# Splitting the second layer's output projection rows during HGRN2's last head

## The chip, the cores and the metric

The kernel runs on one core of one Trainium2 chip. The metric is the device time of one execution in microseconds, as the median of several. The core's engines run side by side and wait for one another through semaphores: TensorE (PE, with its weight loads shown apart as PEld), VectorE (DVE), ScalarE (ACT), GpSimd (POOL), and SyncE (SP), which here only issues DMAs.

## What is computed

A trunk of two layers on 1024 tokens of width 1024, all in float32. Layer 0 has an RWKV-7 and an RG-LRU mixer; layer 1 has HGRN2. After each mixer comes an output projection with a residual add, and then a mixture of experts. The change lies where layer 1's mixer ends and its output projection begins:

```python
def hgrn2_mixer(hn, w_in, lower_bound, norm_w, w_out):
    q, f, i, g = jnp.split(hn @ w_in, 4, axis=-1)
    ...
    o = gla_chunkwise(split_heads(q, HGRN_HEADS), split_heads(k, HGRN_HEADS),
                      split_heads(i, HGRN_HEADS), split_heads(log_f, HGRN_HEADS))
    o = o * lax.rsqrt(jnp.mean(o * o, -1, keepdims=True) + RMS_EPS)
    o = o.reshape(b, s, HGRN_WIDTH) * norm_w * jax.nn.silu(g.astype(jnp.float32))
    return o.astype(hn.dtype) @ w_out

# layer 1
x = x + hgrn2_mixer(hn, c_w_in[j], lbs[layer], c_norm_w[j], c_w_out[j])
hn = rmsnorm(x, norm_ffn[layer])
x = x + hier_moe(hn, ...)
```

## The kernel before, in words

Every large product is made from three products in the fp32r format: each operand is split into a high part (a cast on ACT) and a low part (operand minus high part, a subtraction on DVE), and PE adds high x high, high x low and low x high into one PSUM bank. A weight row block of 128 x 1024 costs one cast and one subtraction.

The program is a row of phases (`phase`), each with one block of five instruction streams, one for each engine. The next block's streams begin when the streams of the last one have ended. Within an engine the order is that of the code. Two phases matter here.

**`hgrn`** (layer 1's mixer) handles 8 heads. For each head, PE computes the four projections q, f, i, g of the normed input `h_T` (high part) and `h_low` (low part) with the head's weight columns. SP fetches these to `w_tiles`, ACT and DVE split them to `w_high` and `w_low`. `step` handles the rest of a head: the products within chunks on seven levels (`level_gram`; DVE makes the exponents with `diff`, ACT exponentiates them with `level_exp`, DVE scales with `scale` and picks results with `pick`), then the transposes of `k_to_end` (`turn`, L2050), the products of keys and values (L2078), the chain of states on DVE (L2315), the output products (L2087, L2088), the square on ACT (L2178), the sums of squares (L2093), their mean on DVE (L2324), a logarithm and an exponential on ACT (L2183, L2184), and two products on DVE (L2331, L2336), the last of which writes the head's rows of `y_T`. While a head goes through `step`, PE fills its waits with the projections of the following head: `project(n)` issues 3n of these matmuls. In the last head (`more` is False) there is no following head, so `project` issues nothing, and neither `w_tiles`, `w_high`, `w_low` nor `h_T`, `h_low` are read any more.

**`moe`** with layer 1's arguments starts with the output projection. SP issues eight DMAs for the rows of `c_w_out` (L1326, to `w_raw`), alternating with eight for the rows of the residual (L1328), and then the norm's gain (L1329) and the router's weights and biases (L1330 to L1333). ACT casts the first 128 tokens of `y_T` (`y_part`, L1440) and then the eight weight row blocks to `wo_high` (L1529); DVE makes the low parts (L1718 and L1780). PE's `project(t, h)` computes half h of the projected token tile t with 24 matmuls (L1574): eight high x high, eight x_low x high, eight x high x low. In tile 0, half 0, it waits for each row block as it comes. Then each tile's result is added to the residual (`add`, L1725, whose first one also waits for the gain), squared on ACT, normed (`rows`, L1730), turned on PE (`turn_rows`, L1595) and multiplied by the router's weights (`logits`, L1605). PE's order is `project(0,0)`, `project(0,1)`, `project(1,0)`, `turn_rows(0)`, `project(1,1)`, `logits(0)`, and so on, up to tile 7. The routing and the experts follow.

Layer 0's `moe` has the same code with one difference (`early`): its output projection rows are already in SBUF, so SP begins with the residual's DMAs. The splits are still made in the phase.

The line of `moe` that holds PE's first tile to the rows:

```python
if t == 0 and h == 0 and ready is not None:
    pe.wait_ge(ready, k + 1)
```

## Time and profile before

| what | us |
|---|---|
| median of 3 runs | 2879.13 (2876.95 to 2888.28) |
| the profiled execution, own time | 2883.18 |
| its span, first to last instruction | 2881.4 |
| PE busy in the span | 2555.6 (89%) |
| DVE busy | 1927.9 (67%) |
| ACT busy | 1603.9 (56%) |

Times in the profile are measured from the span's start. "Idle before" in brackets is the time the engine had nothing to do before the row's instruction, with what ended it; a name ending in q is the engine's own instruction queue, which stands for a semaphore wait.
### The profile page before, as it was taken

How to read it: one execution, taken by the hardware profiler on the slowest of the kernel's cores; microseconds unless marked ns; L12 is line 12 of the kernel's file. 1: busy time of each engine (PE TensorE's matmuls, PEld its weight loads, DVE VectorE, ACT ScalarE, POOL GpSimd, SP SyncE). 2: the span in 40 equal slices, each digit the busy share in tenths (PEclk: the TensorE clock that was granted, in tenths of full speed). 3: DMA queues.
4: the chain of work that ended last, by engine and by line, in shares of the span. 5: the costliest groups of instructions: out<-in, count | busy, mean ns of one | idle time of the engine just before them, and what ended most of it. 6: DMA issues, size and time to landing. Idle time of an engine off the chain costs nothing. (4 is left out here: it accounts for less than half of the span.)

```text
span 2881.4 us, 57941 instructions
## 1 busy us (share of the span) xinstructions
PE 2555.6 (89%) x20860; PEld 2090.6 (73%) x20860; DVE 1927.9 (67%) x2201; ACT 1603.9 (56%) x1867; POOL 379.6 (13%) x342
## 2 busy tenths in 40 slices
PE   5998899979989999999568999997597999999990
PEld 4776799847768888888457777776485788888870
DVE  3358356534479999999545666666335899999974
ACT  3656223253248888888324655554222788888861
POOL 0020000000013333333010000000000122222220
PEclk9999999989989999999779999998797999999995
DMA  3111000013269999999520111110323899999964
GB/s 95 45 44 30 27 4 4 4 60 127 88 231 377 385 382 383 382 375 378 198 72 26 36 38 37 32 31 9 141 75 123 329 376 376 382 383 387 381 256 188
DMA packets 219991, 525.39 MB, mean 182 GB/s; under 512 B 43824, under 2 KB 99120, under 8 KB 219824
## 3 DMA queue, kind: packets, MB, share of 16 engines
q1 hardware_dynamic: 201392, 489.34, 45.8%
q0 software_dynamic: 18432, 33.60, 3.1%
q8 instruction: 132, 2.16, 0.3%
q14 instruction: 35, 0.29, 0.0%
HBM read 506.06 MB, written 50.33 MB: 193 GB/s over the span
## 5 line engine op out<-in xcount | busy, mean ns | idle before, releaser
L1751 DVE TENSOR_TENSOR w_low<-w_raw,w_high 128x1024 fp32r<-128x1024 f32 x768 | 894.8, 1219 | 31.3 <-DVEq L52 21.7
L1464 ACT CAST w_high<-w_raw 128x1024 fp32r<-128x1024 f32 x768 | 755.1, 1049 | 109.1 <-ACTq L52 108.7
L1619 PE MATMUL ps<-w_high,x_high 128*128 128x512 f32 x1024 | 415.0, 405 | 7.5 <-PEq L52 6.6
L1623 PE MATMUL ps<-w_high,x_low 128*128 128x512 f32 x1024 | 404.0, 395 | 0.0
L1622 PE MATMUL ps<-w_low,x_high 128*128 128x512 f32 x1024 | 401.9, 393 | 0.0
L1619 PEld LDWEIGHTS ps<-w_high,x_high 128*128 128x128 f32 x1024 | 195.5, 191 | 50.6 <-issue 14.0
L1623 PEld LDWEIGHTS ps<-w_high,x_low 128*128 128x128 f32 x1024 | 194.2, 190 | 43.4
L2013 PE MATMUL ps<-h_high,w_high 128*128 128x512 f32 x512 | 213.4, 417 | 10.8 <-PEq L52 10.5
L1622 PEld LDWEIGHTS ps<-w_low,x_high 128*128 128x128 f32 x1024 | 195.0, 190 | 37.7
L1619 PE MATMUL ps<-w_high,hidden_high 128*128 128x512 f32 x512 | 200.7, 392 | 6.7 <-PEq L52 6.7
L2013 PE MATMUL ps<-h_high,w_low 128*128 128x512 f32 x512 | 201.9, 394 | 0.0
L2013 PE MATMUL ps<-h_low,w_high 128*128 128x512 f32 x512 | 201.7, 394 | 0.0
L1623 PE MATMUL ps<-w_high,hidden_low 128*128 128x512 f32 x512 | 200.5, 392 | 0.0
L1622 PE MATMUL ps<-w_low,hidden_high 128*128 128x512 f32 x512 | 200.4, 391 | 0.0
L1410 POOL COPY row_index<-place_of_row 128x1 int32 (+1 forms) x64 | 104.2, 1629 | 676.7 <-POOLq L52 676.7
L1469 ACT CAST x_high<-ps 128x1024 fp32r<-128x1024 f32 x64 | 65.0, 1016 | 182.3 <-ACTq L52 182.3
L1412 POOL DMA_INDIRECT expert_rows<-y_rows,row_index x64 | 155.2, 2425 | 56.4 <-POOLq L52 56.4
L263 PE MATMUL ps<-h_high,w_high 128*128 128x512 f32 x352 | 143.2, 407 | 15.5 <-DVE w_low L527 10.8
L1755 DVE TENSOR_TENSOR x_low<-ps,x_high 128x1024 fp32r<-128x1024 f32 x64 | 78.4, 1224 | 105.4 <-DVEq L52 105.4
L263 PE MATMUL ps<-h_high,w_low 128*128 128x512 f32 x352 | 140.5, 399 | 0.0
L263 PE MATMUL ps<-h_low,w_high 128*128 128x512 f32 x352 | 139.9, 397 | 0.0
L1379 POOL IOTA iota_moe<- 128x128 f32 x2 | 0.5, 238 | 1035.2 <-POOLq L1975 559.7
(402 smaller groups left out, 4865.6 us busy)
## 6 DMA issues: line engine op xcount, KB each, us to landing
w_raw<-in_moe_w_gate SPq DMA_DIRECT2D x256, 512.0 KB, 5.2
w_raw<-in_moe_w_up SPq DMA_DIRECT2D x256, 512.0 KB, 5.6
w_raw<-in_moe_w_down SPq DMA_DIRECT2D x256, 512.0 KB
w_raw<-expert_rows SPq DMA_DIRECT2D x32, 512.0 KB, 9.1
w_tiles<-in_c_w_in SPq DMA_DIRECT2D x32, 512.0 KB, 4.0
w_tiles<-in_ab_w_in SPq DMA_DIRECT2D x22, 512.0 KB, 3.9
residual<-in_x SPq DMA_DIRECT2D x16, 512.0 KB, 7.3
h_rows<-hn_moe SPq DMA_DIRECT2D x16, 512.0 KB, 2.9
```

The costliest lines, as they stand in the source:

```text
L263: last = pe.matmul(ps[:, bank(i) + h, :], wx_[:, i % 2, q, :], hx[:, q, tok], start=n == 0, stop=n == len(parts) - 1)
L1379: ch(pool.iota(it, [[1, P]], base=0, channel_multiplier=0, allow_small_or_imprecise_dtypes=True))
L1410: pool.tensor_copy(idx[:, 1:2], dst_row[:, b]).then_inc(order_p, 1)
L1412: pool.indirect_dma_start(c.ys, bass.IndirectOffsetOnAxis(ap=idx[:, 1:2], axis=0), yb, None, bounds_check=2 * S - 1, oob_is_err=False).the ...
L1464: act.copy(wh[:, p, :], raw[:, p, :]).then_inc(high_made, 1)
L1469: act.copy(xh[:, q], ps[:, B_X:B_X + 2, :].rearrange("p b (k n) -> p (b k) n", k=4)).then_inc(order_a, 1)
L1619: ins = pe.matmul(ps[:, bank, :], high, w_h, start=first, stop=False)
L1622: pe.matmul(ps[:, bank, :], high, w_l, start=False, stop=False)
L1623: return pe.matmul(ps[:, bank, :], low, w_h, start=False, stop=final)
L1751: dve.tensor_tensor(wl[:, p, :], raw[:, p, :], wh[:, p, :].bitcast(F32), ALU.subtract).then_inc(low_made, 1)
L1755: dve.tensor_tensor(xl[:, q], ps[:, B_X:B_X + 2, :].rearrange("p b (k n) -> p (b k) n", k=4), xh[:, q].bitcast(F32), ALU.subtract).then_in ...
L2013: last = pe.matmul(ps[:, 2 * (m % 2) + h, :], wx[:, m % 2, k, :], hx[:, k, tok], start=n == 0, stop=n == len(parts) - 1)
```

## The change

`hgrn` gets `w_out`. A ring of five row buffers (`w_out_ring`) is laid over `w_tiles`, `w_high` and `w_low`. PE signals `w_dead` with the first transpose of the last head's v, which comes after the last projection matmul; SP then fetches the rows 0 to 4, and the rows 5 to 7 as their slots come free (after the low part of rows 0 to 2). In the last head's `step`, ACT casts the rows at seven places to the high part, into `h_T`, and DVE makes the low parts at two places, into `h_low`. `moe` takes these two tensors (`split`) in place of `wo_high` and `wo_low`, and neither fetches, splits nor waits for rows. In the last head, `project` now issues one float32 matmul of 128 x 512 into PSUM bank 0, whose result nobody reads, at each of its 12 places.

```diff
--- before.py
+++ after.py
@@ -1202,7 +1202,7 @@
 
-def moe(nc, c, a, layer, y, w_out, next_gain, fetch=None, early=False, h_high=None, h_low=None, out=None):
+def moe(nc, c, a, layer, y, w_out, next_gain, fetch=None, early=False, split=None, h_high=None, h_low=None, out=None):
 
@@ -1279,6 +1279,8 @@
         w_rows = c.w_out_rows if early else raw
+        if split is not None:
+            wo_h, wo_l = split
         at_pos, reach, at_blk = at["at_pos"], at["reach"], at["at_block"]
@@ -1322,7 +1324,7 @@
                 for k in range(KT):
-                    if not early:
+                    if not early and split is None:
                         sp.dma_start(raw[:, k, :], w_out[k * P:(k + 1) * P, :]).then_inc(raw_in[k], 16)
@@ -1334,7 +1336,8 @@
                     sp.dma_start(c.rows[t * P:(t + 1) * P, :], hn[:, t % 2, :]).then_inc(rows_in[t % 2], 16)
-                    sp.wait_ge(wo_low, t + 1)
+                    if split is None:
+                        sp.wait_ge(wo_low, t + 1)
                     load(slice(0, 1), [t], fresh=True)
@@ -1521,7 +1524,7 @@
                 y_part(0)
-                for k in range(KT):
+                for k in range(KT if split is None else 0):
                     if early:
@@ -1569,7 +1572,7 @@
                         for k in range(KT):
-                            if t == 0 and h == 0 and ready is not None:
+                            if t == 0 and h == 0 and ready is not None and split is None:
                                 pe.wait_ge(ready, k + 1)
@@ -1775,7 +1778,7 @@
                 y_rest(0)
-                for k in range(KT):
+                for k in range(KT if split is None else 0):
                     dve.wait_ge(wo_high, k + 1)
@@ -1911,7 +1914,7 @@
 
-def hgrn(nc, c, w, lower_bound, norm_w, h_T, h_low, y_T):
+def hgrn(nc, c, w, lower_bound, norm_w, h_T, h_low, y_T, w_out):
 
@@ -1932,8 +1935,14 @@
         gram_done, gram_free = [sem("gram_done0"), sem("gram_done1")], [sem("gram_free0"), sem("gram_free1")]
+
+        RING = 5
+        with nc.sbuf_tensor("w_out_ring", [P, RING, D], F32) as ring:
+            pass
         wt = sb("w_tiles", [P, KT, P])
         wh, wl = sb("w_high", [P, 2, KT, P], F32R), sb("w_low", [P, 2, KT, P], F32R)
+        w_dead, out_high, out_low = sem("w_dead"), sem("out_high"), sem("out_low")
+        out_in = [sem(f"out_in{k}") for k in range(KT)]
         Q, G, V, F = c.head_rows
@@ -1998,6 +2007,11 @@
                 sp.wait_ge(s["par_in"], 48)
+                sp.wait_ge(w_dead, 1)
+                for k in range(KT):
+                    if k >= RING:
+                        sp.wait_ge(out_low, k - RING + 1)
+                    sp.dma_start(ring[:, k % RING, :], w_out[k * P:(k + 1) * P, :]).then_inc(out_in[k], 16)
 
@@ -2045,20 +2059,27 @@
 
-                def turn(src, done):
+                def turn(src, done, first=None):
                     for n in range(TT):
                         last = pe.transpose(ps[:, 6 + n // 4, (n % 4) * P:(n % 4 + 1) * P], src[:, n * P:(n + 1) * P], c.ident[:])
+                        if n == 0 and first is not None:
+                            last.then_inc(first, 1)
                     last.then_inc(done, 1)
 
-                def turn_v(par):
+                def turn_v(par, first=None):
                     take(pe, s["v_ready"])
                     take(pe, s["tail_free"])
-                    turn(V[:, par, :], s["v_turned"])
-
-                def step(par, more):
+                    turn(V[:, par, :], s["v_turned"], first)
+
+                def step(par, more, final=False):
                     ahead = projection() if more else iter(())
+                    if not more:
+                        take(pe, bank_free[0])
 
                     def project(n):
+                        if not more:
+
+                            pe.matmul(ps[:, 0, :], c.ident[:], Q[:, par, 0:HALF], start=True, stop=True)
                         for _ in range(3 * n):
@@ -2094,7 +2115,7 @@
                     if more:
-                        turn_v(1 - par)
+                        turn_v(1 - par, w_dead if final else None)
 
@@ -2102,7 +2123,7 @@
                     step(1, True)
-                step(0, True)
+                step(0, True, final=True)
                 step(1, False)
@@ -2150,23 +2171,36 @@
 
+                def row_high(*ks):
+                    for k in ks:
+                        act.wait_ge(out_in[k], 16)
+                        act.copy(h_T[:, k, :], ring[:, k % RING, :]).then_inc(out_high, 1)
+
                 def step(par, more, ahead=True):
...
                     level_exp(4)
+                    if not more:
+                        row_high(0)
                     level_exp(5)
+                    if not more:
+                        row_high(1)
                     if more:
...
                         level_exp(lv)
+                    if not more:
+                        row_high(2)
                     take(act, s["diff_ready"])
...
                         high(3)
+                    if not more:
+                        row_high(3, 4)
                     take(act, s["kd_turned"])
@@ -2174,8 +2208,12 @@
                             high(0)
+                    if not more:
+                        row_high(5, 6)
                     take(act, s["o_done"])
                     act.activation(KD[:], pair(ps[:, 4:6, :]), ACT.Square).then_inc(s["sq_ready"], 1)
+                    if not more:
+                        row_high(7)
                     if more:
@@ -2285,6 +2323,11 @@
 
+                def row_low(*ks):
+                    for k in ks:
+                        dve.wait_ge(out_high, k + 1)
+                        dve.tensor_tensor(h_low[:, k, :], ring[:, k % RING, :], h_T[:, k, :].bitcast(F32), ALU.subtract).then_inc(out_low, 1)
+
                 def step(h, par, more, ahead=True):
@@ -2309,6 +2352,8 @@
                     dve.tensor_tensor(QE[:], QE[:], Q[:, par, :], ALU.mult).then_inc(s["qe_ready"], 1)
+                    if not more:
+                        row_low(0, 1)
                     take(dve, s["ds_done"])
@@ -2320,6 +2365,8 @@
                             low(0)
+                    if not more:
+                        row_low(*range(2, KT))
                     take(dve, s["sq_summed"])
@@ -2394,8 +2441,8 @@
         with nc.sbuf_tensor("hgrn_y_h", [P, 3 * KT, S], F32):
-            hgrn(nc, c, a["c_w_in"][0], a["c_lower_bound"], a["c_norm_w"][0], h_T, h_low, y_T)
-        moe(nc, c, a, 1, y_T[:], a["c_w_out"][0], a["norm_final"], fetch=c.res_rows, out=out)
+            hgrn(nc, c, a["c_w_in"][0], a["c_lower_bound"], a["c_norm_w"][0], h_T, h_low, y_T, a["c_w_out"][0])
+        moe(nc, c, a, 1, y_T[:], a["c_w_out"][0], a["norm_final"], fetch=c.res_rows, split=(h_T, h_low), out=out)
         with nc.Block() as block:
...
```

Where instructions move, in three places.

PE, last head of `hgrn` (v, q, k, level_ops, k_to_end, v_rows, scores_T and states are that head's tensors; the row of `q,ident` is the new matmul). Before:

```order
L2024 MATMUL ps<-q,k 128x128 x8
L2038 MATMUL ps<-level_ops 64x64 x8
L2038 MATMUL ps<-level_ops 32x32 x16
L2044 MATMUL ps<-level_ops 32x16 x160
L2050 MATMUL ps<-ident,k_to_end 128x128 x8
L2078 MATMUL ps<-v_rows,k_rows 128x128 x8
L2087 MATMUL ps<-scores_T,v_rows 128x128
```

and with the change, in two pieces (between them the pattern of level and new matmul repeats):

```order
L2038 MATMUL ps<-q,k 128x128 x8
L2082 MATMUL ps<-q,ident 128x512
L2052 MATMUL ps<-level_ops 64x64 x8
L2082 MATMUL ps<-q,ident 128x512
L2052 MATMUL ps<-level_ops 32x32 x16
L2082 MATMUL ps<-q,ident 128x512
L2058 MATMUL ps<-level_ops 32x16 x32
```

```order
L2082 MATMUL ps<-q,ident 128x512
L2064 MATMUL ps<-ident,k_to_end 128x128 x8
L2082 MATMUL ps<-q,ident 128x512
L2099 MATMUL ps<-v_rows,k_rows 128x128 x8
L2082 MATMUL ps<-q,ident 128x512
L2108 MATMUL ps<-scores_T,v_rows 128x128
```

A new matmul now stands before each level, before the transposes, before the key-value products and before the output products; two more stand before and behind the sums of squares.

ACT, from the last head's level exponentials to the next phase. Before:

```order
L2165 ACTIVATE k_to_end<-k_to_end 128x1024
L2166 ACTIVATE q_from_start<-cum_log_f 128x1024
L2171 COPY k_rows<-ps 128x1024
L2178 ACTIVATE k_to_end<-ps 128x1024
L2183 ACT_TABLE_LOAD
L2183 ACTIVATE log_f<-log_f 128x1024
L2184 ACT_TABLE_LOAD
L2184 ACTIVATE log_f<-log_f 128x1024
L1975 UNCONDITIONAL_BRANCH
L1435 UNCONDITIONAL_BRANCH
L1440 CAST x_high<-y_T 128x1024
L1529 CAST wo_high_moe<-w_raw 128x1024 x8
```

and with the change:

```order
L2177 CAST h_high<-w_out_ring 128x1024
L2197 ACTIVATE k_to_end<-k_to_end 128x1024
L2198 ACTIVATE q_from_start<-cum_log_f 128x1024
L2177 CAST h_high<-w_out_ring 128x1024 x2
L2205 COPY k_rows<-ps 128x1024
L2177 CAST h_high<-w_out_ring 128x1024 x2
L2214 ACTIVATE k_to_end<-ps 128x1024
L2177 CAST h_high<-w_out_ring 128x1024
L2221 ACT_TABLE_LOAD
```

The eight casts have moved ahead of the block's end; the first two of them stand still further ahead, between level exponentials.

DVE, the same stretch. Before:

```order
L2311 TENSOR_TENSOR q_from_start<-q_from_start,q 128x1024
L2315 SCALAR_TENSOR_TENSOR states<-states,step_decay,ps 128x128 x7
L2324 TENSOR_SCALAR log_f<-ps 128x1024
L2331 SCALAR_TENSOR_TENSOR log_f<-ps,norm_w,log_f 128x1024
L2336 TENSOR_TENSOR y_T<-log_f,g 128x1024
L1975 UNCONDITIONAL_BRANCH
L1706 UNCONDITIONAL_BRANCH
L1718 TENSOR_TENSOR x_low<-y_T,x_high 128x1024
L1780 TENSOR_TENSOR wo_low_moe<-w_raw,wo_high_moe 128x1024 x8
```

and with the change:

```order
L2354 TENSOR_TENSOR q_from_start<-q_from_start,q 128x1024
L2329 TENSOR_TENSOR h_low<-w_out_ring,h_high 128x1024 x2
L2360 SCALAR_TENSOR_TENSOR states<-states,step_decay,ps 128x128 x7
L2329 TENSOR_TENSOR h_low<-w_out_ring,h_high 128x1024 x6
L2371 TENSOR_SCALAR log_f<-ps 128x1024
```

Two subtractions now stand ahead of the chain of states, six behind it and ahead of the mean of squares.

## Rows read from the trace of the kernel before

**Rows 1.** Timeline of PE, the output projection of layer 1: start, duration, row

```profile
2047.44 0.76 PE L1574 MATMUL ps<-wo_high_moe,x_high 128*128 128x512 f32 x1 [14.94 <-ACT wo_high_moe L1529]
...
2065.28 0.79 PE L1574 MATMUL ps<-wo_high_moe,x_high 128*128 128x512 f32 x1 [1.78 <-ACT wo_high_moe L1529]
...
2070.62 1.98 PE L1574 MATMUL ps<-wo_high_moe,x_high 128*128 128x512 f32 x8
...
2076.06 1.98 PE L1574 MATMUL ps<-wo_high_moe,x_high 128*128 128x512 f32 x8
...
2081.51 1.03 PE L1595 MATMUL ps<-ident,hn_moe 128*128 128x128 f32 x8
```

**Rows 2.** Timelines of SP, DVE and ACT, start of layer 1's `moe`

```profile
2042.52 0.35 SPq L1326 DMA_DIRECT2D w_raw<-in_c_w_out  x1
...
2043.62 1.23 DVE L1718 TENSOR_TENSOR x_low<-y_T,x_high 128x1024 fp32r<-128x1024 f32 x1 [1.59 <-ACT x_high L1440]
...
2048.82 1.04 ACT L1529 CAST wo_high_moe<-w_raw 128x1024 fp32r<-128x1024 f32 x1 [1.53 <-ACTq L52]
```

**Rows 3.** Stretches: length, busy us (instructions) of PE, PEld, DVE, ACT, POOL, PEclk, DMA share, GB/s

```profile
2023.50:2027.00 3.50, 3.17 (x15) 3.20 (x16) 0.00 (x0) 0.00 (x0) 0.00 (x0) 0.50 0.02 5
2046.00:2065.00 19.00, 5.52 (x7) 2.00 (x7) 8.58 (x7) 8.13 (x8) 0.59 (x1) 0.50 1.03 413
2068.00:2071.00 3.00, 3.00 (x14) 2.48 (x13) 0.12 (x1) 0.00 (x0) 0.00 (x0) 0.97 0.04 6
2226.40:2231.90 5.50, 5.50 (x13) 4.32 (x14) 1.23 (x1) 1.07 (x2) 0.00 (x0) 0.50 0.17 60
```

**Rows 4.** Layer 0's `moe`, first transfers and first add (timelines of SP and DVE)

```profile
651.86 3.93 SPq L1328 DMA_DIRECT2D residual<-in_x  x8
...
666.99 0.69 DVE L1725 TENSOR_TENSOR residual<-residual,ps 128x512 f32<-128x512 f32 x1 [2.50 <-DMA gain_rows_moe<-in_norm_ffn]
```

**Rows 5.** Timeline of PE, the last head

```profile
2011.52 1.06 PE L2044 MATMUL ps<-level_ops 128*32 128x16 f32 x64 [2.21 <-PEq L52]
2012.51 1.97 PE L2050 MATMUL ps<-ident,k_to_end 128*128 128x128 f32 x8
2015.75 3.75 PE L2078 MATMUL ps<-v_rows,k_rows 128*128 128x128 f32 x16 [1.27 <-PEq L52]
2023.83 0.77 PE L2087 MATMUL ps<-scores_T,v_rows 128*128 128x128 f32 x2 [4.33 <-PEq L52]
...
2030.54 1.95 PE L2093 MATMUL ps<-k_to_end,ones 128*128 128x512 f32 x4 [1.29 <-PEq L52]
```

**Rows 6.** Timelines of ACT and DVE, the last head

```profile
2005.94 0.69 ACT L2136 ACTIVATE level_ops<-level_ops 128x512 f32<-128x512 f32 x1 [1.80 <-ACTq L52]
2029.38 1.02 ACT L2178 ACTIVATE k_to_end<-ps 128x1024 f32<-128x1024 f32 x1 [13.77 <-ACTq L52]
...
2019.77 3.31 DVE L2315 SCALAR_TENSOR_TENSOR states<-states,step_decay,ps 128x128 f32<-128x128 f32 x7 [2.99 <-DVEq L52]
2032.65 1.22 DVE L2324 TENSOR_SCALAR log_f<-ps 128x1024 f32<-128x1024 f32 x1 [9.57 <-DVEq L52]
```

**Rows 7.** The page's DMA issues: KB each, median us from issue to landing

```profile
w_tiles<-in_c_w_in SPq DMA_DIRECT2D x32, 512.0 KB, 4.0
```

**Rows 8.** Timeline of PE: float32 matmuls of 128 x 512, and a level product, elsewhere

```profile
625.47 1.91 PE L786 MATMUL ps<-residual,head_ones 128*128 128x512 f32 x2
...
1937.87 0.74 PE L2044 MATMUL ps<-level_ops 128*32 128x16 f32 x64
...
2188.31 10.46 PE L1677 MATMUL ps<-residual,ones 128*128 128x512 f32 x24
```

**Rows 9.** Stretches with PE partly busy (columns as in rows 3)

```profile
617.00:621.00 4.00, 1.49 (x4) 0.68 (x4) 2.13 (x3) 3.94 (x5) 0.00 (x0) 0.99 0.00 0
621.00:622.00 1.00, 1.00 (x2) 0.00 (x0) 0.06 (x1) 1.00 (x1) 0.00 (x0) 0.50 0.00 0
644.80:648.00 3.20, 1.48 (x4) 0.38 (x2) 2.19 (x3) 3.15 (x4) 0.00 (x0) 1.00 0.00 0
```

## The prediction

> **What bounds the kernel now.** The page gives PE 89% of the span, so I first ask where PE waits, and read the waits by engine for the stretch around the change. The largest of PE there stands in [rows 1]: the projection of layer 1 starts at 2047.44 after 14.94 us of idleness, and its first eight matmuls then come one by one, the last at 2065.28, each released by a cast. Only from 2065.28 does PE run densely; the second half of tile 0 starts at 2070.62 and tile 1 at 2076.06. Then I read ACT and DVE. ACT's casts take 1.04 us and stand 1.53 us idle before each, waiting for a queue [rows 2]. The table of stretches says what they wait for: from 2046 to 2065 the DMA engines are fully busy at 413 GB/s, PE is busy for 5.52 of 19 us and its clock is at the lower level [rows 3]. So the start of the projection is bound by the transfer of 4.2 MB of weight rows, which alternate with 4.2 MB of residual. The first tile's operand is ready much earlier, at 2043.62 + 1.23 = 2044.85 [rows 2]. From 2076 on PE is dense, and everything behind it (router, experts) is started by what PE and the norm deliver.
>
> The other half of the change lies in the last head. There PE waits for DVE and ACT (idle 2.21 us before a level product of 1.06 us), so each of the last levels takes the 3.27 us that DVE needs [rows 5]. From 2012.51 the head is a chain of PE, ACT and DVE in turn [rows 5, 6]: transposes, copy, key-value products (to 2019.5), states (to 2023.1), output products (to 2029.3), square, sums (to 2032.5), mean. Any delay in it delays the phase's end.
>
> **Step 1, the projection's start.** Fetch, casts and subtractions leave the phase. PE can start when the operand is split, 2044.95. Half a tile is 24 matmuls; at the upper clock they cost 2076.06 - 2070.62 = 5.44 us [rows 1], tile 0 therefore 10.9 us. The clock is at the lower level at the start, since PE has been idle for over 10 us. How long it stays there I take from three places: dense from 2065.28, at the upper level for nearly all of 2068 to 2071 (about 2.8 us); dense from 2023.5, lower until 2027.0 (3.5 us); dense from 2226.4, lower for all of 5.5 us [rows 3]. A matmul takes about twice as long there, so c us at the lower level cost c/2. With the middle of 2.8 and 5.5, c = 4.2: tile 0 takes 13.0 us, and tile 1 starts at 2057.95 where it started at 2076.06. **Saving 18.1 us**, between 17.4 (c = 5.5) and 18.8 (c = 2.8).
>
> What is late next? The first add waits for the gain, which is queued behind the residual. Layer 0 has just this order of transfers without weight rows: first issue 651.86, the add released by the gain at 666.99, 15.1 us later [rows 4]. Here the first issue is at 2042.52 [rows 2], so the first add starts at 2057.65 and ends at 2058.35, 0.4 us after tile 0's second half is done. PE needs the normed rows only for its transposes behind the first half of tile 1, which came without a wait at 2081.51 [rows 1], 5.45 us after tile 1's start. That path has a few tenths of slack, so I take **0.1 us** of loss, between 0 and 1. The router's weights and biases stand behind the gain in the queue; the logits need them only after tile 1's second half, at about 2069, some 11 us after the gain, so I cost them at nothing.
>
> **Step 2, casts and subtractions in the last head.** Costs are 1.04 us each on ACT and 1.22 us on DVE. The rows 0 to 4 are asked for at 1986, when v's transposes begin, and land some 4 us later [rows 7], long before the first cast at about 2001. ACT idles 1.80 us between level exponentials and 13.77 us before the square [rows 6], so the first seven casts are covered: nothing. DVE idles 2.99 us before the states and 9.57 us before the mean [rows 6]: two subtractions (2.4 us) fit in the first gap, six (7.4 us) in the second. Rows 5, 6 and 7 are asked for when their slots are free, at about 2018, 2019 and 2024; with 4 us they land by 2022, 2023 and 2028. The cast of row 7 stands behind the square (2030.4), its subtraction ends at 2032.7, against 2032.65 for the mean now. Cost 0.1 us while the head keeps its pace; if the head gets faster, row 7 takes some of that gain.
>
> **Step 3, the twelve added matmuls.** One is two instructions: 0.87 us at the upper clock (10.46 us for 24 instructions), 1.7 us at the lower (two in 1.91 us, which includes the fill) [rows 8]. Seven stand before the levels, where PE idles 2.21 us [rows 5]: covered, even at 1.9. The eighth stands between the last level and the transposes, which now start without a gap at 2012.51 [rows 5]; it is exposed in full. The ninth has 1.27 us of cover, the tenth 4.33, the eleventh 1.29 [rows 5], the twelfth delays nobody. What they do to the clock decides. Now it is at the lower level until 2027.0 [rows 3], and the whole of this chain up to the output products runs there.
>
> - Clock stays up: the last level's product takes 0.74 us instead of 1.06 and ends 0.3 us sooner, the eighth matmul takes 0.87, the transposes 1.0 instead of 1.97, the key-value products 1.9 instead of 3.75 [rows 5], done at 2017.4. Now DVE's two subtractions are late next: they end at 2019.2, so states start 0.5 us sooner than 2019.77. The output products take 3.8 us instead of 5.5 (2023.83 to 2029.38 [rows 5, 6]), together 2.1 us sooner. Row 7's subtraction (landing 2028, cast, 1.2 us) gives back 0.3: **1.8 us gained**.
> - Clock falls as before: the eighth matmul costs 1.7 and the ninth 0.4, against a clock that opens sooner behind the denser run from 2011.5. Between 1.1 gained and 2.1 lost; I take 0.6 lost.
>
> In the stretch from 617 to 621 PE was busy 37% of the time and the clock was at the lower level right after it, from 621; from 644.8 to 648 it was busy 46% and the clock stayed up [rows 9]. With the new matmuls a level of 3.27 us holds 0.87 + 0.74 us of PE [rows 8], 49%, though almost half of that in tiles of 32 columns. That is above both rows, so I take the clock as staying up. The page "TensorE: Matmul & The Clock Gate" of the Trainium skill (section "HAM oscillation — how this bites in real kernels") puts the fall down to idle gaps alone. The row from 617 disagrees in part, since PE was idle for only 2.5 of its 4 us; by the page the sum is that of the first case, by that row the second has to be reckoned with.
>
> **Sum.** 18.1 - 0.1 + 1.8 = 19.8 us. The profiled execution took 2883.18 us and so comes to 2863.4. It lies 4.05 us above the median of the runs; from 2879.13 the same saving gives **2859.3 us**.
>
> **Rivals.**
> - *A, the forecast*: 2859.3, between 2858.0 (18.8 + 2.3) and 2861.
> - *B, the clock falls in the last head*: 18.1 - 0.1 - 0.6 = 17.4, 2861.7; ends 15.3 and 19.8, so 2859.3 to 2863.8. For it speaks the row from 617 and that the level products use narrow tiles; against it the row from 644.8.
> - *C, the transfers at the phase's head decide*: gain or router weights land 3 to 6 us later than in layer 0, because reading back the residual is slower than reading x. PE then waits before its transposes, and the saving is 12 to 15: 2864 to 2867. Against it: 413 GB/s was reached here with the same transfers in the mix.
> - *D, the change hides what was hidden*: if the experts' first weights or the routing set the end of the stage by a clock of their own, the 18 us vanish and 2877 to 2880 remains. Against it: each of these loads is issued by a wait on the normed rows, so it moves along.
> - *E, slower*: the ring. Row 7 is asked for at 2024 by the end of row 2's subtraction, and the mean waits behind its subtraction on DVE. A landing of L us costs L - 6, and the change turns slower when L exceeds 6 + 18 = 24 us; a landing of 40 would give 2895. Against it: a landing of 4 us in this phase with the queue empty, as it is here [rows 7].
>
> **How the numbers follow.** Chances: A 0.50, B 0.35, C 0.07, D 0.06, E 0.02. A saving over 0.5% is one over 14.4 us, about what a measurement of this kernel can tell from no change. A and B save 15 to 21, but the runs of before spread over 11 us, so the measured medians may put a saving of 17 below the bound; I leave 0.06 of A and B for that, and 0.02 of C above it. Faster 0.81, within 0.5% 0.17, slower 0.02. The range takes in A and B with their ends (2858.0 to 2863.8), 4 us below for the spread of the runs' median (2876.95 is the fastest run before), and above as far as C: 2854 to 2868.
>
> **What would show it.** Right: first projection matmul some 3 us after the last row of `y_T` and 24 dense ones behind it; PEclk 1.00 through the levels; the mean of squares 1.5 to 2 us sooner than 2032.65; no idle PE before the first transposes of the normed rows. B shows as PEclk 0.50 in the levels. C shows as an add released by the gain and idle PE behind tile 1's first half. Wrong: a wait of ACT or DVE for rows inside the head, or a time between 2872 and 2880.

## The result, and the profile after

The change made the kernel faster by about 0.6%, as forecast: the median of 5 runs is 2864.53 us (2860.32 to 2867.0) against 2881.68 us (2876.95 to 2888.28, 5 runs) for the kernel before. The ratio is 0.994, with a 95% interval of 0.9927 to 0.9954, and the medians differ by 17.15 us. The forecast was a saving of 19.8 us and 2859.3 us; the measured time lies in the range of 2854 to 2868.

The interval of the ratio is some 8 us wide, and unchanged code alone moves by several us between two executions: up to v's transposes of the last head the profiled execution before took 1985.77 us, the one after 1989.64. So I split each profiled execution at marks that every kernel has:

- the **head**: from the start of the last head's v transposes to the end of the last `y_T` row;
- the **start**: from there to tile 1's first projection matmul; the first transposes of normed rows follow 5.45 us later unless PE has to wait.

| us | before | after | difference |
|---|---|---|---|
| up to the last head | 1985.77 | 1989.64 | +3.87 |
| head | 56.27 | 56.09 | -0.18 |
| start | 34.02 | 15.49 | -18.53 |
| tile 1 to the span's end | 805.34 | 803.68 | -1.66 |
| span | 2881.4 | 2864.9 | -16.5 |

What the change touches saved 18.7 us; the other two rows are code that is the same in both kernels.

The timeline of PE after the change, from the last level of the last head to the first transposes of normed rows (start, duration, row), answers to [rows 1, 5]:

```profile
2015.43 0.73 PE L2058 MATMUL ps<-level_ops 128*32 128x16 f32 x64 [1.49 <-PEq L52]
2016.08 1.13 PE L2082 MATMUL ps<-q,ident 128*128 128x512 f32 x2
2017.04 1.04 PE L2064 MATMUL ps<-ident,k_to_end 128*128 128x128 f32 x8
2017.92 1.02 PE L2082 MATMUL ps<-q,ident 128*128 128x512 f32 x2
2019.36 2.02 PE L2099 MATMUL ps<-v_rows,k_rows 128*128 128x128 f32 x16 [0.41 <-PEq L52]
2021.21 1.02 PE L2082 MATMUL ps<-q,ident 128*128 128x512 f32 x2
2026.94 0.77 PE L2108 MATMUL ps<-scores_T,v_rows 128*128 128x128 f32 x2 [4.70 <-PEq L52]
...
2048.59 3.68 PE L1577 MATMUL ps<-h_high,x_high 128*128 128x512 f32 x8 [11.54 <-DVE x_low L1721]
2052.11 2.02 PE L1577 MATMUL ps<-h_high,x_low 128*128 128x512 f32 x8
...
2061.22 1.98 PE L1577 MATMUL ps<-h_high,x_high 128*128 128x512 f32 x8
...
2066.67 1.03 PE L1598 MATMUL ps<-ident,hn_moe 128*128 128x128 f32 x8
```

The projection now waits for its operand alone and runs its 24 matmuls of each half in a row; the first eight take 3.5 us at the lower clock, then the short ones begin. Up to the key-value products the head runs at the upper clock (1.04 and 2.02 us, against 1.97 and 3.75 in [rows 5]). Then PE idles for 4.70 us, and the first pair of output products takes 0.77 us as before.

DVE and ACT after the change, the same stretch (answers to [rows 2, 4, 6]):

```profile
2020.61 2.35 DVE L2329 TENSOR_TENSOR h_low<-w_out_ring,h_high 128x1024 fp32r<-128x1024 f32 x2
2022.88 3.30 DVE L2360 SCALAR_TENSOR_TENSOR states<-states,step_decay,ps 128x128 f32<-128x128 f32 x7
...
2035.06 1.22 DVE L2329 TENSOR_TENSOR h_low<-w_out_ring,h_high 128x1024 fp32r<-128x1024 f32 x1 [2.86 <-ACT h_high L2177]
2036.34 1.23 DVE L2371 TENSOR_SCALAR log_f<-ps 128x1024 f32<-128x1024 f32 x1
...
2060.88 1.28 DVE L1728 TENSOR_TENSOR residual<-residual,ps 128x512 f32<-128x512 f32 x2 [11.12 <-DMA gain_rows_moe<-in_norm_ffn]
```

```profile
2025.20 1.04 ACT L2177 CAST h_high<-w_out_ring 128x1024 fp32r<-128x1024 f32 x1 [5.99 <-DMA w_out_ring<-in_c_w_out]
2027.78 1.05 ACT L2177 CAST h_high<-w_out_ring 128x1024 fp32r<-128x1024 f32 x1 [1.53 <-DMA w_out_ring<-in_c_w_out]
2033.07 1.02 ACT L2214 ACTIVATE k_to_end<-ps 128x1024 f32<-128x1024 f32 x1 [4.25 <-ACTq L52]
```

The states start behind two low parts, without a gap: DVE, not the key-value products (done at 2021.4), now sets their start. ACT waits for rows 5 and 6, but has 4.25 us to spare before the square. Row 7 has nothing to spare: its low part ends at 2036.28, PE's sums of squares at 2036.19, and the mean starts at 2036.34. The first add waits for the gain, until 15.15 us after `y_T`, and PE's transposes come without a wait all the same.

The stretches of the head (columns as in [rows 3]) show the clock:

```profile
2016.00:2020.00 4.00, 3.58 (x36) 2.23 (x25) 3.30 (x4) 2.01 (x3) 0.00 (x0) 1.00 0.00 0
2020.00:2024.00 4.00, 2.24 (x15) 1.41 (x13) 3.71 (x6) 0.00 (x0) 0.00 (x0) 1.00 0.23 67
2024.00:2028.00 4.00, 1.06 (x5) 1.09 (x6) 3.17 (x7) 1.27 (x2) 0.00 (x0) 0.59 0.57 196
2028.00:2032.00 4.00, 4.00 (x22) 4.00 (x22) 4.00 (x4) 0.82 (x1) 0.00 (x0) 0.56 0.42 135
```

It is up through the levels and the key-value products, and falls soon after 2024, in PE's idle gap behind them. That it stayed up through the levels is not certain even with the twelve added matmuls, as the section on e8 shows.

### The profile page after: what moved, and what is told of

Same layout as the page of the kernel before. It is cut to its first block and busy times, and to the rows that moved or that the text cites. A ratio compares the mean times of both kernels' runs of the same rounds, so it can differ in the third digit from the quotient of the medians.

```text
span 2864.9 us, 57992 instructions
## 1 busy us (share of the span) xinstructions
PE 2560.0 (89%) x20884; PEld 2091.0 (73%) x20884; DVE 1927.5 (67%) x2201; ACT 1603.4 (56%) x1867; POOL 381.3 (13%) x342
```

## The experiments

The profiled head, start and time up to the first transposes, by the marks above, with the ratio to the kernel before and its 95% interval:

| kernel | ratio | head | start | to transposes |
|---|---|---|---|---|
| before | 1 | 56.27 | 34.02 | 39.47 |
| the change | 0.994 (0.9927 to 0.9954) | 56.09 | 15.49 | 20.94 |
| e1 no added matmuls | 0.994 (0.9927 to 0.9953) | 57.31 | 15.77 | 21.22 |
| e2 added matmuls alone | 0.9998 (0.9989 to 1.0008) | 55.52 | 34.61 | 40.06 |
| e3 rows' transfers first | 0.9966 (0.9953 to 0.9979) | 56.52 | 26.32 | 31.76 |
| e4 three more matmuls | 0.9937 (0.9922 to 0.9951) | 55.52 | 15.76 | 21.21 |
| e5 filler up to the start | 0.9924 (0.9907 to 0.994) | 54.42 | 17.02 | 22.47 |
| e6 e5, gain first | 0.9928 (0.9914 to 0.9941) | 54.07 | 15.81 | 21.26 |
| e7 one low part ahead | 0.9921 (0.9901 to 0.9942) | 54.39 | 16.03 | 21.48 |
| e8 low parts on GpSimd | 0.9935 (0.9919 to 0.9951) | 61.48 | 15.44 | 21.30 |
| e9 fetch alone | 0.9957 (0.9943 to 0.997) | 57.40 | 20.72 | 26.17 |
| e10 low parts behind | 0.9922 (0.9909 to 0.9936) | 52.75 | 16.77 | 22.21 |
| e11 e10 and the start | 0.9929 (0.9915 to 0.9942) | 52.72 | 13.91 | 19.35 |
| e12 e10's order, no filler | 0.9933 (0.992 to 0.9946) | 57.34 | 15.76 | 21.42 |

An interval is 0.2 to 0.4% wide, 5 to 12 us. So the times tell the change from before and from e2. The interval of e3 only touches that of the change, that of e9 overlaps it, and the variants of the head can't be told from one another. Those are read from the profiles, one of each, and there a head can differ by about a microsecond for how long the clock was down alone: with the same output products and no added matmul, it took 56.27 (before), 56.52 (e3), 57.31 (e1), 57.34 (e12) and 57.40 us (e9).

### e1: the change without the added matmuls

```diff
                     def project(n):
-                        if not more:
-
-                            pe.matmul(ps[:, 0, :], c.ident[:], Q[:, par, 0:HALF], start=True, stop=True)
                         for _ in range(3 * n):
```

> The change without its twelve added matmuls; everything else stays. Two stretches are read in the profile: the head (from the start of v's transposes to the end of the last y_T row, 56.3 us before, 56.1 with the change) and the start (from there to tile 1's first projection matmul, 34.0 before, 15.5 with the change). Theory: the gain is all in the start, so the start stays at 15 to 16 us and the total stays within 1 us of the change's. The head then runs its levels at the lower clock as before: 56.3 to 56.9. Rival (the added matmuls carry part of the gain by keeping the clock up): the head gets longer by 1.8 us or more, 57.9 or above.

The ratio is that of the change. The head ran as before up to its output products (states at 2015.42, 33.9 us after v's transposes; 34.0 before), with five casts and two low parts already done. From the square on it took 12.66 us, as before, so the other casts and low parts are covered too. Between the two it took 6.66 us from the first output product to the square, where the kernel before took 5.55 and the change 6.13. That is the clock, which in e1 opened 5.7 us after the dense run began and before it opened after 3.2. So the theory's 56.3 to 56.9 was passed by 0.4, and the rival's 57.9 not reached. The head with the added matmuls is 1.2 us shorter in this pair of profiles, but kernels without them differ by as much among themselves (56.27 to 57.40), and the times show nothing.

### e2: the added matmuls alone, in the kernel before

```diff
+                    if not more:
+                        take(pe, bank_free[0])
                     def project(n):
+                        if not more:
+                            pe.matmul(ps[:, 0, :], c.ident[:], Q[:, par, 0:HALF], start=True, stop=True)
                         for _ in range(3 * n):
```

> The kernel before plus only the twelve added matmuls. The start must stay at 34 us in every theory. Theory (the clock falls in the gap before the output products because DVE's two subtractions and the states keep PE idle there): without the subtractions DVE is ready for the states sooner, PE's idle gap is about 1.5 us shorter; if that is enough to keep the clock up, the head takes 56.3 - 2.1 - 1.5 = 52.5 to 53.5; if not, the states still come sooner and the head takes 54 to 55. Rival (the added matmuls give nothing by themselves): 56 to 57.

PE's timeline in e2:

```profile
2010.43 2.02 PE L2083 MATMUL ps<-v_rows,k_rows 128*128 128x128 f32 x16 [0.41 <-PEq L52]
2012.29 1.02 PE L2066 MATMUL ps<-q,ident 128*128 128x512 f32 x2
2016.81 0.77 PE L2092 MATMUL ps<-scores_T,v_rows 128*128 128x128 f32 x2 [3.50 <-PEq L52]
```

The output products start 36.1 us after v's transposes, 1.2 sooner than with the change (37.3): without the two low parts DVE begins the states sooner. PE still idles for 3.50 us and still comes back at the lower clock, and stays there for 5.7 us, so of 2 us gained ahead of the output products 0.75 remain: the head takes 55.52, between theory (55 at most) and rival. In the times nothing is seen (0.9998).

### e3: the weight rows' transfers ahead of the residual's, in the kernel before

```diff
                 for k in range(KT):
                     if not early:
                         sp.dma_start(raw[:, k, :], w_out[k * P:(k + 1) * P, :]).then_inc(raw_in[k], 16)
+                for k in range(KT):
                     if fetch is not None:
```

> The kernel before with the eight weight row transfers issued ahead of the eight residual transfers, nothing else. If the start is bound by the transfer, rows land every 1.3 us in place of 2.56, the eighth by about 2055, tile 0 ends some 10 us sooner; the gain is still behind all 8.4 MB (landing at 2067) and holds the first add. So the start shrinks from 34.0 to 24 to 25 us, and PE then waits about 1 to 2 us before its first transposes: total 8 to 9 us less, half of what the change gives. Rival (the casts and subtractions in the phase cost the time, not the transfer): the start stays within 2 us of 34.

The casts of the rows in e3, against 1.53 us of idleness before each in [rows 2]:

```profile
2048.22 1.04 ACT L1530 CAST wo_high_moe<-w_raw 128x1024 fp32r<-128x1024 f32 x1 [0.22 <-ACTq L52]
2049.50 1.04 ACT L1530 CAST wo_high_moe<-w_raw 128x1024 fp32r<-128x1024 f32 x1 [0.24 <-ACTq L52]
```

Rows now come about every 1.3 us. The start shrank by 7.7 us, to 26.32 where 24 to 25 was expected; a microsecond of that is the clock, since from the last row's first matmul to tile 1 it took 11.77 us in place of 10.78. The run shrank by 0.34%, somewhat over half of what the change gives, from one line of order. So the transfer bound the start, and a good part of that was that a row waited behind residual that nobody needed yet. The wait for the gain was there (the first add at 25.36 us, released by it), but cost PE nothing: the transposes came 5.44 us after tile 1's start.

### e9: the fetch alone

```diff
+                sp.wait_ge(w_dead, 1)
+                for k in range(KT):
+                    sp.dma_start(c.raw_rows[:, k, :], w_out[k * P:(k + 1) * P, :]).then_inc(c.w_out_in[k], 16)
...
-        w_rows = c.w_out_rows if early else raw
+        w_rows = c.w_out_rows if early else raw if rows_at is None else rows_at[:]
```

> The kernel before with only the fetch moved: all eight rows are fetched during the last head into SBUF that is no longer read (the low part of the normed input), and cast and subtracted in the next phase as before; no added matmuls. Theory: the change's gain in the start is mostly the transfer. The start is then like layer 0's, where the rows are in SBUF too: about 20.6 us from y_T to tile 1 (34.0 before, 15.5 with the change), so the moved fetch is worth 13.4 us and the moved splits the other 5. The head stays at 56.3 to 57.4. Rival (splits and transfer are equally binding, so the fetch alone gives little): 28 us or more.

20.72 us, against 20.6 read from layer 0. So of the 18.5 us in the start the moved fetch brings 13.3 and the moved splits 5.2. With the rows in SBUF, ACT's casts set the pace (one matmul every 0.95 us):

```profile
2047.63 0.79 PE L1574 MATMUL ps<-wo_high_moe,x_high 128*128 128x512 f32 x1 [0.15 <-ACT wo_high_moe L1529]
2048.58 0.79 PE L1574 MATMUL ps<-wo_high_moe,x_high 128*128 128x512 f32 x1 [0.15 <-ACT wo_high_moe L1529]
```

### e4: three more matmuls ahead of the output products

```diff
+                    for _ in range(3 if not more else 0):
+                        pe.matmul(ps[:, 0, :], c.ident[:], Q[:, par, 0:HALF], start=True, stop=True)
                     take(pe, s["s_ready"])
```

> The change plus three more of the added matmuls ahead of the last head's output products. Theory (the output products ran at the lower clock because PE idled 4.7 us before them): the idle gap shrinks to about 2 us, PEclk stays 1.00, the output products take 3.8 us in place of 6.0, and row 7's fetch and cast become late: the head takes 54.3 to 55 us in place of 56.1. Rival (row 7's fetch bounds the mean of squares anyway): the head stays at 55.8 or above. The start stays at 15 to 16 us in both.

```profile
2022.37 0.46 PE L2110 MATMUL ps<-scores_T,v_rows 128*128 128x128 f32 x2 [2.14 <-PEq L52]
2022.67 0.39 PE L2111 MATMUL ps<-q_from_start,states 128*128 128x128 f32 x2
...
2023.34 0.43 PE L2110 MATMUL ps<-scores_T,v_rows 128*128 128x128 f32 x2
2023.56 0.64 PE L2111 MATMUL ps<-q_from_start,states 128*128 128x128 f32 x2
...
2026.98 0.39 PE L2111 MATMUL ps<-q_from_start,states 128*128 128x128 f32 x2
```

The clock was still up when the output products began, and fell in their midst at 2023.5, 1.2 us after PE had come back from only 2.14 us of idleness, to be up again at 2026.98: 5.56 us for them, the head 55.52, and the theory's 54.3 to 55 missed. PE had not idled since, so I take the fall to answer, late, to the idleness before; no run here excludes another cause. e8 shows the same: after 3.47 us of idleness its output products began at the upper clock at 2027.87 and turned slow at 2028.39. The page "TensorE: Matmul & The Clock Gate" of the Trainium skill (section "HAM oscillation — how this bites in real kernels") tells of it as a wait that is followed by a cold run. Here a run that began warm turned cold while it was dense.

### e7: one low part ahead of the states

```diff
-                        row_low(0, 1)
+                        row_low(0)
...
-                        row_low(*range(2, KT))
+                        row_low(*range(1, KT))
```

> The change with one subtraction in place of two ahead of the last head's chain of states, the other behind it. Theory (with the clock up the key-value products are done 1.5 us before DVE is): the states start about 1.1 us sooner, 32.1 us after v's transposes in place of 33.2, and the idle gap of PE before the output products shrinks to 3.5 us; row 6 and row 7 land later but before they're needed, so the head takes 54.7 to 55.3 us, if the clock opens within the output products at the same point. Rival (a later fetch of rows 6 and 7 takes the gain): 55.9 or more, with ACT waiting for a row in front of the square.

States at 32.08 us after v's transposes, as forecast. With an idle gap of 3.57 us in place of 4.70 the clock stayed up this time, and the output products took 3.8 us. The rival holds too: row 6 was asked for later, ACT stood before it, and the square behind it (the output products were done at 2028.17, so it could have begun at 2028.3):

```profile
2029.01 1.04 ACT L2177 CAST h_high<-w_out_ring 128x1024 fp32r<-128x1024 f32 x1 [4.18 <-DMA w_out_ring<-in_c_w_out]
2029.96 1.02 ACT L2214 ACTIVATE k_to_end<-ps 128x1024 f32<-128x1024 f32 x1
```

Of 3.4 us gained ahead of the square 1.7 were given back there; the head took 54.39, a little below the expected 54.7 to 55.3, which had not counted on the clock.

### e8: the low parts of rows 0 to 2 on GpSimd

```diff
+                for k in range(3):
+                    pool.wait_ge(out_high, k + 1)
+                    pool.tensor_tensor(h_low[:, k, :], ring[:, k, :], h_T[:, k, :].bitcast(F32), ALU.subtract).then_inc(pool_low, 1)
...
-                        sp.wait_ge(out_low, k - RING + 1)
+                        sp.wait_ge(pool_low, k - RING + 1)
...
-                        row_low(0, 1)
...
-                        row_low(*range(2, KT))
+                        row_low(*range(3, KT))
```

> The change with the low parts of rows 0, 1 and 2 made by GpSimd, as soon as ACT has cast them, in place of DVE; SP waits for these for the rows 5 to 7, and DVE makes the low parts of rows 3 to 7 behind the states. Theory (DVE's order sets the states and the fetch of the last rows): the states start right after the key-value products, 31.7 to 32.0 us after v's transposes; rows 5 to 7 are in SBUF before the output products begin, and nothing waits for them; head 53.5 to 55. Rival (GpSimd's subtractions slow DVE's in the levels, where DVE is fully busy): the levels take longer than 3.27 us each, and the head takes 56 or more.

The rival, and far beyond it: the head took 61.48 us. GpSimd and DVE in e8:

```profile
2000.64 3.00 POOL L1992 TENSOR_TENSOR h_low<-w_out_ring,h_high 128x1024 fp32r<-128x1024 f32 x1 [519.61 <-ACT h_high L2180]
2004.01 2.38 POOL L1992 TENSOR_TENSOR h_low<-w_out_ring,h_high 128x1024 fp32r<-128x1024 f32 x1 [0.37 <-ACT h_high L2180]
```

```profile
1998.66 0.68 DVE L2309 TENSOR_TENSOR level_ops<-level_ops,k 128x512 f32<-128x512 f32 x1
...
2001.33 0.73 DVE L2294 COPY_PREDICATED scores_T<-level_masks,ps 128x512 f32<-128x512 uint32 x1
2001.93 2.26 DVE L2309 TENSOR_TENSOR level_ops<-level_ops,k 128x512 f32<-128x512 f32 x1
2004.43 2.50 DVE L2314 TENSOR_TENSOR level_ops<-level_ops,q 128x512 f32<-128x512 f32 x1 [0.24 <-DVEq L52]
```

A DVE multiplication that takes 0.68 us takes 2.26, 2.50 and, at the third subtraction, 2.25 us when it meets GpSimd, and ends 0.54 to 0.56 us after the end of GpSimd's instruction each time, however long they overlap: it looks like a wait, not a slowdown. The copy ahead of the first, which reads PSUM and one SBUF tensor, takes its usual 0.73. The three lengthened multiplications cost DVE 5.0 us. The page "GPSIMD Engine Reference" of the Trainium skill (section "Key points") says that the two engines share their SBUF interfaces, with contention for DVE instructions that have two SBUF inputs. The rows agree, and show its size.

The rest of the head's loss is the clock, and it fell in the levels, before GpSimd did anything. PE in e8:

```profile
1997.30 0.87 PE L2061 MATMUL ps<-level_ops 128*32 128x16 f32 x64 [3.15 <-PEq L52]
1998.09 2.08 PE L2085 MATMUL ps<-q,ident 128*128 128x512 f32 x2
...
2018.20 1.92 PE L2067 MATMUL ps<-ident,k_to_end 128*128 128x128 f32 x8
```

The added matmul takes 2.08 us in place of 1.12 at 1998.09, GpSimd's first subtraction starts at 2000.64. The transposes are cold too (1.92 us, 1.04 in the change), and the states start 39.19 us after v's transposes, 7.2 us later than where nothing of DVE stands in front of them (e2, 32.01): 5.0 for GpSimd, some 2.2 for the lower clock. The same fall is in the levels of e5, e6, e7, e10 and e11, whose code is that of the change up to there: for 6 to 14 us their added matmuls took up to 2.08 us and their level products up to 1.06. There the clock was up again before the transposes and the states started no later for it, since DVE sets the pace of the levels. Only in the change, e2 and e4 was it up all through. So of nine profiles with the added matmuls, six have the fall that they were meant to prevent.

### e10: low parts behind the states and behind the mean

```diff
-                        row_low(0, 1)
+                        row_low(0)
...
-                        row_low(*range(2, KT))
+                        row_low(*range(1, 6))
...
                     dve.sem_inc(s["tail_free"], 1)
+                    if not more:
+                        row_low(6, 7)
...
-                        row_high(5, 6)
+                        row_high(5)
...
-                        row_high(7)
+                        row_high(6, 7)
...
+                    for _ in range(3 if not more else 0):
+                        pe.matmul(ps[:, 0, :], c.ident[:], Q[:, par, 0:HALF], start=True, stop=True)
                     take(pe, s["s_ready"])
```

> The change with another order in the last head: one low part ahead of the states, those of rows 1 to 5 behind them, those of rows 6 and 7 behind the mean of squares, where DVE idles 5.2 us; ACT casts row 5 ahead of the square, rows 6 and 7 behind it; and three more added matmuls ahead of the output products. Theory: states start 32.1 us after v's transposes, output products 36.1 to 40.0 at the upper clock, nothing of ACT or DVE waits for a row, the mean of squares comes at 43.3, and the head takes 52.6 to 53 us (56.1 with the change): 3.3 us less in total. Rival (something else in the tail binds, such as ACT's casts ahead of the logarithm): 54 or more.

States at 32.1 us, output products at 36.17, square at 40.10, mean at 43.37, head 52.75: each within 0.15 us of the forecast, 3.3 less than with the change. ACT did wait for rows 5 and 7 (6.04 and 0.55 us), which cost nothing. DVE in e10:

```profile
2018.79 5.76 DVE L2331 TENSOR_TENSOR h_low<-w_out_ring,h_high 128x1024 fp32r<-128x1024 f32 x5 [0.24 <-DVEq L52]
2026.51 1.22 DVE L2373 TENSOR_SCALAR log_f<-ps 128x1024 f32<-128x1024 f32 x1 [1.96 <-DVEq L52]
2028.07 2.36 DVE L2331 TENSOR_TENSOR h_low<-w_out_ring,h_high 128x1024 fp32r<-128x1024 f32 x2 [0.33 <-DVEq L52]
2032.94 1.28 DVE L2382 SCALAR_TENSOR_TENSOR log_f<-ps,norm_w,log_f 128x1024 f32<-128x1024 f32 x1 [2.51 <-DVEq L52]
```

The mean waits for PE's sums alone, and the last two low parts lie in DVE's wait for ACT's logarithm and exponential. In the times, 2855.5 us (2852.45 to 2860.06) and 0.9922; the interval overlaps that of the change.

### e12: e10's order without filler

Against e10:

```diff
                     def project(n):
-                        if not more:
-
-                            pe.matmul(ps[:, 0, :], c.ident[:], Q[:, par, 0:HALF], start=True, stop=True)
                         for _ in range(3 * n):
...
-                    for _ in range(3 if not more else 0):
-                        pe.matmul(ps[:, 0, :], c.ident[:], Q[:, par, 0:HALF], start=True, stop=True)
                     take(pe, s["s_ready"])
```

> e10's order of casts and low parts, without any added matmul. Theory (order and filler act together: at the lower clock the key-value products end 33.7 us after v's transposes, after DVE's lows in either order, so the order alone frees nothing): states start at 33.9 to 34.0 as before, output products at 38.0, and the head takes 56.3 to 57.4 us as in e1, the spread being how long the output products stay at the lower clock; total within 0.1% of e1's ratio 0.994. Rival (the order alone carries e10's gain): head 54 or less.

The head took 57.34 us, like e1's 57.31. At the lower clock the key-value products end at 33.7 us, and DVE is done by then with what stands ahead of the states, two low parts in e1 or one here. So the order pays only with the filler. The filler hardly pays with twelve matmuls or fifteen (the change, e4), but in the change's own order, with six more ahead of the output products and no gap left there, the head takes 54.42 and 54.07 (e5, e6, next section): the states start at 33.2 as with the change, and the output products take 3.9 us. The gain over the change there is the clock alone; e10's is clock and order.

### e5, e6 and e11: keeping the clock up for the projection

e5, against the change:

```diff
                     project(8)
+                    for _ in range(6 if not more else 0):
+                        pe.matmul(ps[:, 0, :], c.ident[:], Q[:, par, 0:HALF], start=True, stop=True)
                     take(pe, s["s_ready"])
...
                     project(9)
+                    for _ in range(7 if not more else 0):
+                        pe.matmul(ps[:, 0, :], c.ident[:], Q[:, par, 0:HALF], start=True, stop=True)
...
+                for _ in range(3 if split is not None else 0):
+                    pe.matmul(ps[:, 2, :], c.ones[:], y[:, 0, 0:HALF], start=True, stop=True)
                 for t in range(TT):
                     project(t, 0)
```

e6, against e5; e11 makes the same edit to e10 and adds the last two loops of the diff above, with 9 and 2 matmuls in place of 7 and 3:

```diff
+                if split is not None:
+                    sp.dma_start(gb, gain.partition_broadcast(P)).then_inc(gain_in, 16)
                 for k in range(KT):
...
-                sp.dma_start(gb, gain.partition_broadcast(P)).then_inc(gain_in, 16)
+                if split is None:
+                    sp.dma_start(gb, gain.partition_broadcast(P)).then_inc(gain_in, 16)
```

> The change plus added matmuls in every longer idle stretch of PE up to the projection: six ahead of the output products (e4 had three), seven behind the sums of squares, three at the head of the next phase. Theory (what the output products and tile 0 lose at the lower clock is given back by filler, but the gain's transfer is late next): the head takes 54.0 to 54.8 us; tile 0's matmuls take 10.9 us in place of 12.6, but the first add still waits for the gain (about 15 us after the residual's first issue), so the normed rows come late and PE idles 1 to 2 us before its first transposes. From the end of y_T to those transposes: 20.3 to 21 us against 20.94 with the change. Rival (the gain has slack): this stretch shrinks to 19.3.

> e5 plus the gain's transfer issued ahead of the residual's in layer 1. Theory: the wait for the gain is gone, and the stretch from the end of y_T to the first transposes takes 19.0 to 19.4 us with no idle PE in it; head as in e5; total 3 us below the change's. Rival (the first residual rows then hold the add, or the clock isn't held over the phases' border): 20.5 or more.

> e10 plus nine added matmuls behind the sums of squares and two at the head of the next phase (e5 and e6 had seven and three, which let the clock fall in a gap of 3.2 us and then ran into the projection's start), and the gain's transfer first. Theory: the clock stays up over the phases' border, the first projection matmul comes 2.9 us after y_T, tile 0 takes 10.9 us, so the start takes 13.8 to 14.0 us and the stretch to the first transposes 19.2; total 5 us less than the change. Rival (the border's gap lets the clock fall all the same): 15.5 to 17 for the start.

PE's timeline where the head ends and the next phase begins, in e6, then in e11:

```profile
2030.51 6.17 PE L2125 MATMUL ps<-q,ident 128*128 128x512 f32 x14
2039.89 4.51 PE L1674 MATMUL ps<-y_T,ones 128*128 128x512 f32 x6 [3.20 <-PEq L1989]
2043.83 2.42 PE L1580 MATMUL ps<-h_high,x_high 128*128 128x512 f32 x8
```

```profile
2026.75 7.89 PE L2125 MATMUL ps<-q,ident 128*128 128x512 f32 x18
2036.13 1.95 PE L1674 MATMUL ps<-y_T,ones 128*128 128x512 f32 x4 [1.49 <-PEq L1989]
2038.46 2.11 PE L1580 MATMUL ps<-h_high,x_high 128*128 128x512 f32 x8 [0.38 <-DVE x_low L1726]
```

In e5 and e6 PE idled for 3.20 us at the border, the clock fell, and the three filler matmuls, now 1.8 (e5) and 1.5 us (e6) each in place of 0.87, delayed the first projection matmul by 2.1 us in e5 and 1.6 us in e6 (5.01 and 4.48 us after `y_T`, against 2.86): both expectations missed for this stretch, e6 went by its rival (21.26 us to the transposes), and the start cost 17.02 and 15.81 us. Only the head gained as expected (54.42 and 54.07). In e11 the gap was 1.49 us, the clock stayed up, the first projection matmul waited for its operand alone, and the start took 13.91 us: 2.9 for the operand, 11.0 for tile 0. There the first add was released by PE (8.73 us after `y_T`), not by the gain. Head and start together took 66.63 us in e11, against 71.58 with the change and 90.29 before. In the times the 5 us do not show: 2856.13 us (2853.5 to 2858.14) and 0.9929, beside e10's 2855.5 and 0.9922.

## Why the prediction was right

**Step 1, the projection's start** (18.1 us, between 17.4 and 18.8) measured 18.5. The three terms came out one by one: the first matmul 2.86 us after `y_T`; 3.5 us or so at the lower clock where I had taken 4.2, the middle of the shortest and longest of three places; tile 0 in 12.6 where I had 13.0. Over the profiles with this start it varied from 15.44 to 16.77 (change, e1, e4, e7, e8, e10, e12), which is this term alone. That transfer and splits bound the start, and in what parts, is shown by e3 and e9: 13.3 us fetch, 5.2 us splits.

**What is late next**: the gain. It released the first add 15.15 us after `y_T`, and cost PE nothing; I had taken 0.1 us. It becomes a bound where tile 0 is faster or the gain later, which e11 avoids by issuing it first. e5, meant to show the loss, lost its time elsewhere. But e8 shows the onset: there the gain released the first add 15.74 us after `y_T` and tile 1 began at 15.44, and the transposes came 5.86 us behind that in place of 5.45, after the normed rows:

```profile
2067.39 1.10 PE L1598 MATMUL ps<-ident,hn_moe 128*128 128x128 f32 x8 [0.26 <-DVE hn_moe L1733]
```

In e12 they were 0.2 us late (15.86, 15.76 and 5.66 us).

**Step 2, casts and low parts in the last head**: hidden, shown by e1, whose head ran as before up to the output products and from the square on. A "wait of ACT or DVE for rows inside the head" was to be a sign of being wrong, and it came: ACT waited 5.99 and 1.53 us for rows 5 and 6. The sign was too strict, since both waits lie in idleness that ACT had anyway.

**Step 3, the added matmuls**, is where the forecast was too high: 1.8 us gained, 0.2 measured in the pair of profiles. The levels, the transposes and the key-value products ran at the upper clock, as in the forecast A, and the states started 0.8 us sooner (33.24 us after v's transposes, 34.00 before). The mean of squares was to come 1.5 to 2 us sooner and came 0.2 us sooner (46.70, 46.88). The step that failed is "the output products take 3.8 us instead of 5.5". I asked whether the clock holds through the levels and didn't ask it of the next gap, although I had worked out that DVE would make that gap longer. PE idled 4.70 us there, the clock fell, and they took 6.1 us. With the clock up the output products take 3.8 to 3.9 us, as the forecast had it (e5, e6, e7, e10, e11), and the heads of these five are 1.9 to 3.6 us shorter than before.

That the clock stayed up through the levels was partly luck. The forecast took it from PE's busy share alone; with the same code up to there the clock fell in the levels of six of the nine profiles with the added matmuls. In five of these it cost nothing, which rival B had not foreseen, and in e8 some 2 us. What decides it in one execution no run here shows.

The rivals: B's mechanism (the clock falls in the last head) came in the change's profile in another gap than B had it, and in six others in the levels as B had it; its time, 2861.7, is nearer to the measured one than A's. C, D and E didn't come: gain and router weights were in time, the rest of the program moved along, and rows 5 to 7 landed early enough, row 7 without a margin.

Against the median of the runs shown at first, 2879.13, the saving would be 14.6; against the five of the comparison, 2881.68, it is 17.15. The forecast of 19.8, the 17.4 of rival B and the 18.7 of the profiles all lie within the interval (13 to 21 us), so the times agree with step 1 and can't judge step 3. The measured 2864.53 is 5.2 us above the forecast time, and 2.55 of these are only that the median of before came out higher with more runs.

## What to carry to other kernels

Weights that a phase needs first can be fetched and prepared in the tail of the phase before, once you find buffers that are dead there and idle time on the engines that prepare them; read the gain of the fetch and of the preparation separately, since a change of issue order alone may give a good part of it (7.7 of 18.5 us here). Filler matmuls pay where the clock is still up for a dense run on the chain that ends last: here only where the gap in front of it was closed (e5, e6), cut to 1.0 us (e10, e11), or survived once by chance (e7). Where such a gap stays, look for what else sets the start of the dense run, and don't expect the filler to hold the clock in every execution. In a tail where PE, ACT and DVE hand work to one another, side work belongs behind the instruction that others wait for, in the engine's own wait for the next engine.

## What the runs showed that I had not expected

- The clock can fall inside a dense run, 1.2 us after it began, presumably for idleness that lay before it (e4, at 2023.5 after a gap of 2.14 us; e8, 0.5 us after it began), while a gap of 3.57 us was once survived (e7). With one and the same code for them the output products took 5.55, 5.81, 6.66, 6.67 and 6.69 us (before, e3, e1, e12, e9); their matmuls differ only in how long they ran at the lower clock.
- The clock fell in the levels in six of nine profiles with the same twelve added matmuls, mostly without a cost, since DVE set the pace there (e5 to e8, e10, e11).
- GpSimd holds back DVE where both read two SBUF tensors: 0.68 us became 2.25 to 2.50 (e8).
- Unchanged code moves more than many edits: the time up to the last head lay between 1979.55 and 1989.64 us over the profiles, that behind the first transposes between 794.6 and 800.1. The clock is part of it: from about 1632 to 1942 e12 gained 7.2 us on the kernel before, and from 1650 to 1980 the granted clock was 1.00 in e12 and 0.97 to 0.98 before.
